# Token-tile projections of the recurrence first, decay sums at other places, forget operations ahead of the taps

## The chip, the core and the metric

The kernel runs on one core of a Trainium2 chip. The core has a matrix engine (TensorE, PE in the profile, with PEld for its weight loads), three engines for elementwise work (VectorE or DVE, ScalarE or ACT, GpSimd or POOL), and a sync engine (SP) that issues most of the transfers. The metric is the device time of one launch in microseconds (us); lower is better.

## The reference

One layer of a decoder for 512 tokens of width 1024, in float32. What matters here is the first block, the mixer: a normalised input is projected once, and three groups of heads use the columns.

```python
y = h @ w_in                       # h: rmsnorm(x), 512 x 1024
fq, fk, fv, ff, hq, hf, hi, hg, cu, cg = split_columns(y, IN_SIZES)
log_f = log_sigmoid(ff + fox_f_bias)          # 8 heads
fo = forgetting_attention(fq, fk, fv, log_f)  # logits + (cumsum(log_f)[t] - cumsum(log_f)[s])
ho = hgrn2_recurrence(hq, hf, hi, lb)         # S_t = diag(f_t) S_{t-1} + (1-f_t) v_t^T, v = hi
ho = rmsnorm(ho) * silu(hg)
a  = causal_depthwise_conv(cu * sigmoid(cg), conv_w, conv_b)   # 31 taps
co = silu(channel_group_norm(a))
x  = x + concat([fo, ho, co]) @ w_out
```

Behind it come cross attention to 256 memory tokens (their keys and values are `mem_n @ w_xkv`) and a mixture of 16 experts, and a last normalisation.

## The kernel before

Each engine has its own program, written out by hand in program order; engines meet through semaphores. Nothing is scheduled by a tool: an instruction that waits holds up all that stands behind it on its engine. There is one order on PE, and the change edits it.

**The start.** SP issues the four token tiles of x (128 tokens x 1024, 512 KB each), then the small parameter rows, then the weights in slots of 512 columns (2 MB each). For each tile ACT squares and sums it, DVE turns the sum into a mean (L982), POOL takes the root (L646), DVE scales the tile into `n_sb` (L993), PE transposes it in two groups of four 128x128 blocks (`turn_group`, L1533), and DVE copies each group times a gain to `hT` (`turn_evac`, L998). Before the change DVE scales tile t and only then empties the turned tile t-1.

**The projections.** `run` counts the groups g: each takes a PSUM bank (`bank_of(g)`, g % 4 for g < 16), raises `proj` when done, and ACT empties it in the order of the list `PROJ` and raises `proj_out`. `across(slot, col)` makes 128 output columns turned, for all 512 tokens (8 matmuls of 128x512, L1722). `input_and_gates(t)` makes hi and ff (264 columns) for one token tile alone (8 matmuls of 128x264, L1754). Since the data are float32, one matmul stands as two in the profile. In the program before, cu, cg, hq and hf (8 groups `across`) come first and the four `input_and_gates` behind them; then `turned_gates` transposes ff (L1761), then the output gates hg, the queries, keys and values of attention, with the work of the recurrence between them.

**DVE behind the projections.** 62 convolution taps (`conv`, L1291 and L1295, two channel groups of 31) in three portions of 26, 14 and 22, with the recurrence's gates (L1311, L1314) and cumulative sums (L1321 to L1327) behind the first portion and the forget gate's work (L1333 to L1339) behind the second; then the attention masks `att_mask` (L1369) and the states of the recurrence, `states_of(p, t)` (L1360, 8 chained steps each). PE makes the products of state step i in `hgrn_u(i)` (L1808); for i >= 2 it waits until DVE has used those of i-2, as the banks alternate.

**The attention loop.** 16 steps u, of 4 query tiles for each of 4 pairs of heads. Step u: `qk(u)` (L1900, and L1902 for the causal mask), `pv(u-3)` (L1924), `pt(u-2)` (L1911, transposes of probabilities), `cum(h)` at the steps of `CUM_AT` (L1889: one matmul spreads head h's cumulative log decay over 128 rows, in bank 7; DVE copies it out in `f_cum`, L1452), `fox_ms` (L1932) after each pair, and at the steps of `KV_AT` one piece of the projection of the memory (L1722 with Dn, 128x256, or L1732, also in bank 7). Bank 7 serves all three, and `bank7_free` waits for the reader of its last content before the next write.

## Time and profile before

| | us |
|---|---|
| median of 3 timed runs (762.08 to 763.15) | 762.64 |
| profiled execution, its own time | 754.83 |
| its span, first to last instruction | 753.1 |
| PE busy | 697.4 (93%) |
| DVE busy | 276.1 (37%) |
| ACT busy | 146.7 (19%) |
| POOL busy | 64.9 (9%) |

Each engine's busy time lies within the span, so the shares don't add up to one. The chain of work that ended last runs over PE for 88% of the span. The profiled execution took 7.8 us less than the median of the timed runs; 1.7 us of its own time lie outside its span.

### The profile page before, as it was taken

The numbers are of one execution on the slowest core, as the hardware profiler recorded it, in microseconds if no ns is written. First come the engines' busy times: TensorE is split into PE (matmuls) and PEld (weight loads), VectorE is DVE, ScalarE is ACT, GpSimd is POOL, SyncE is SP. The second block draws the span as 40 slices with busy tenths as digits, with TensorE's granted clock in tenths as the row PEclk, the third lists the DMA queues.
The fourth block names the chain that finished last, engine by engine and source line by source line (L and its number), as shares of the span: only waits on it lengthen the run. The fifth ranks groups of instructions, "written<-read, shape, count | busy, mean of one in ns | idle before, by whom it ended". The sixth has DMA issues, their size and how long they took to land.

```text
span 753.1 us, 8347 instructions
## 1 busy us (share of the span) xinstructions
PE 697.4 (93%) x3388; PEld 336.5 (45%) x3388; DVE 276.1 (37%) x646; ACT 146.7 (19%) x304; POOL 64.9 (9%) x94
## 2 busy tenths in 40 slices
PE   4999999999989999999999999999955999999992
PEld 3444745454546565454444446544442333333331
DVE  5046996533043544411220005412151732112147
ACT  3100441004262333311100003300010101011112
POOL 2000090420010000000000000000001000000031
PEclk9999999989999999999999999999985999999997
DMA  8730330302221303110009603030089799999562
GB/s 311 251 111 0 113 111 1 112 1 71 98 88 29 112 1 112 52 61 1 0 0 331 215 13 112 2 131 35 29 283 303 237 351 391 376 378 394 194 224 111
DMA packets 65714, 108.21 MB, mean 144 GB/s; under 512 B 5400, under 2 KB 40460, under 8 KB 65676
## 3 DMA queue, kind: packets, MB, share of 16 engines
q1 hardware_dynamic: 62796, 97.19, 37.0%
q0 software_dynamic: 2880, 10.49, 3.8%
q8 instruction: 27, 0.44, 0.2%
q14 instruction: 11, 0.09, 0.0%
HBM read 98.23 MB, written 9.44 MB: 143 GB/s over the span
## 4 chain that ended last, share of the span: by engine, by line
PE 88%; DVE 6%; ACT 2%; DMA 2%; issue 1%; POOL 0%; DVEq 0%; SPq 0%; POOLq 0%
PE bank L1722 27%; PE bank L1980 15%; PE bank L1587 11%; PE bank L1732 8%; PE bank L1615 6%; PE bank L1754 2%; PE bank L2053 2%; PE bank L1768 2%; PE bank L2033 2%; PE bank L1569 2%; PE bank L1924 2%; PE bank L1900 1%; DVE x_sb L1217 1%; PE bank L1533 1%; PE bank L1911 1%
## 5 line engine op out<-in xcount | busy, mean ns | idle before, releaser
L1722 PE MATMUL bank<-hT,W 128*128 128x512 f32 x384 | 168.4, 598 | 1.8 <-DVE hT L998 1.8
L1722 PEld LDWEIGHTS bank<-hT,W 128*128 128x128 f32 x384 | 72.9, 192 | 93.9 <-issue 91.3
L1980 PE MATMUL bank<-W,n_sb 128*128 128x512 f32 x256 | 111.5, 593 | 0.7 <-ACT n_sb L966 0.7
L1980 PEld LDWEIGHTS bank<-W,n_sb 128*128 128x128 f32 x256 | 48.1, 190 | 59.8 <-issue 58.3
L1587 PE MATMUL bank<-W,A 128*32 128x512 f32 x528 | 72.3, 607 | 1.5 <-DVE A L1152 1.5
L1295 DVE SCALAR_TENSOR_TENSOR A<-A,pc 128x511 f32<-128x511 f32 (+29 forms) x60 | 49.4, 824 | 2.1
L1615 PE MATMUL bank<-Dn,A 128*32 128x512 f32 x384 | 43.7, 595 | 0.5 <-ACT A L772 0.5
L1587 PE MATMUL bank<-hT,A 128*32 128x512 f32 x96 | 42.3, 594 | 0.0
L646 POOL TENSOR_TENSOR rstd<-ss,mhalf 128x1 f32<-128x1 f32 x14 | 7.7, 548 | 382.8 <-DVE ss L982 382.8
L1480 DVE TENSOR_TENSOR x_sb<-x_sb,bank 128x512 f32<-128x512 f32 x16 | 11.0, 687 | 79.7 <-PE bank L1980 79.7
L1587 PEld LDWEIGHTS bank<-W,A 128*32 128x32 f32 x528 | 19.2, 112 | 42.6 <-issue 40.4
L1722 PE MATMUL bank<-Dn,W 128*128 128x256 f32 x128 | 33.0, 416 | 4.1 <-DVE A L1452 3.9
L833 ACT ACTIVATE A<-bank 128x512 f32<-128x512 f32 (+1 forms) x22 | 12.2, 556 | 112.0 <-PE bank L1722 91.9
L1161 DVE TENSOR_TENSOR A<-A,bank 128x256 f32<-128x256 f32 x12 | 5.0, 421 | 75.6 <-ACT A L765 75.5
L1722 PEld LDWEIGHTS bank<-Dn,W 128*128 128x128 f32 x128 | 26.0, 208 | 12.4 <-DVE A L1452 8.4
L1420 DVE CUSTOM_DVE_ANT_0 hT<-bank,A 128x128 f32<-128x128 f32 (+3 forms) x32 | 14.4, 487 | 43.2 <-PE bank L1902 43.1
L1732 PE MATMUL bank<-W,hT 128*128 128x512 f32 x64 | 29.9, 623 | 0.0
L1495 DVE TENSOR_REDUCE fmx<-bank 128x1 f32<-128x256 f32 x16 | 6.7, 420 | 62.4 <-PE bank L2033 62.3
L1732 PE MATMUL bank<-W,Dn 128*128 128x512 f32 x64 | 28.2, 594 | 0.0
L743 ACT ACTIVATE A<-x_sb 128x1024 f32<-128x1024 f32 x8 | 8.5, 1057 | 95.8 <-DVE x_sb L1480 95.8
L1360 DVE SCALAR_TENSOR_TENSOR states<-states,Dn,bank 128x64 f32<-128x64 f32 x64 | 18.0, 281 | 19.7 <-PE bank L1808 17.2
L765 ACT ACTIVATE A<-bank 128x256 f32<-128x256 f32 x12 | 4.6, 384 | 100.9 <-PE bank L1587 100.9
(287 smaller groups left out, 796.2 us busy)
## 6 DMA issues: line engine op xcount, KB each, us to landing
Dn<-in_w_down_dram SPq DMA_DIRECT2D x16, 1024.0 KB, 12.3
W<-in_w_gate_dram SPq DMA_DIRECT2D x11, 1024.0 KB, 6.5
W<-in_w_up_dram SPq DMA_DIRECT2D x11, 1024.0 KB, 10.6
W<-in_w_in_dram SPq DMA_DIRECT2D x5, 2048.0 KB, 8.7
W<-in_w_xkv_dram SPq DMA_DIRECT2D x4, 2048.0 KB, 8.1
y_dram<-A SPq DMA_DIRECT2D x10, 512.0 KB, 10.9
W<-in_w_out_dram SPq DMA_DIRECT2D x2, 2048.0 KB, 7.7
W<-in_w_xq_dram SPq DMA_DIRECT2D x2, 2048.0 KB, 8.4
```

Source lines behind the costliest of these rows:

```text
L1295: nc.vector.scalar_tensor_tensor(out=y[:, s:S], in0=a[:, 0:S - s], scalar=pc[:, r:r + 1], in1=y[:, s:S], op0=ALU.mult, op1=ALU.add).then_i ...
L1360: nc.vector.scalar_tensor_tensor(out=states[:, k + 1, :], in0=states[:, k, :], scalar=he4[:, p, k * CHUNK + CHUNK - 1:k * CHUNK + CHUNK], ...
L1569: mm = nc.tensor.transpose(PS[k][:, c * P:(c + 1) * P], src[:, b, (4 * k + c) * P:(4 * k + c + 1) * P], identf[:, :])
L1587: mm = nc.tensor.matmul(PS[2 + b][r, :], xgT[:, b, c, r], gu_at[GU_HOME[e]][:, c, :], start=c == 0, stop=c == DC - 1)
L1615: mm = nc.tensor.matmul(PS[5 + n][r, :], hidT[:, p % 2, k, r], Dn[:, DN_HOME[e], k, 512 * n:512 * n + 512], start=k == 0, stop=k == 1)
L1722: mm = nc.tensor.matmul(bank[0:w, 0:n], lhs, src[:, c, 0:n], start=c == 0, stop=c == DC - 1)
L1732: mm = nc.tensor.matmul(bank[:, 0:w], src[:, c, t * P:(t + 1) * P], W[:, slot, c, col:col + w], start=c == 0, stop=c == DC - 1)
L1754: mm = nc.tensor.matmul(bank[:, 0:IW], hT[:, c, t * P:(t + 1) * P], w_if[:, c, :], start=c == 0, stop=c == DC - 1)
L1768: mm = nc.tensor.matmul(bank[:, :], lhs, hT[:, c, :], start=c == 0, stop=c == DC - 1)
L1924: mm = nc.tensor.matmul(PS[6][64 * a:64 * a + 64, i * P:(i + 1) * P], v[:, j, h * FD:(h + 1) * FD], fpT[a][:, j * P:(j + 1) * P], start=j ...
L1980: mm = nc.tensor.matmul(PS[k % 4][:, :], src[:, c, t * P:(t + 1) * P], W[:, (n_load + n) % SLOTS, c, :], start=first and j == 0, stop=last ...
L2033: mm = nc.tensor.matmul(PS[u % 2][:, 0:M], xqT[:, 2 * h + k, t * P:(t + 1) * P], xkT[:, 2 * h + k, :], start=k == 0, stop=k == 1)
```

## The change

Four edits. (1) SP issues the weights of hi and ff right behind the first tile of x. PE projects hi and ff tile by tile, between the transposes, and only then makes cu, cg, hq and hf. DVE empties each turned tile before it scales the next. `PROJ`, `GROUPS` and the counts that others wait for follow. (2) DVE does the forget gate's operations ahead of the second portion of taps. (3) The first two decay sums go to banks 2 and 3 behind the third group of values, and not to bank 7 in front of the loop; later ones stand right behind `qk`, and their copies on DVE ahead of the copy of `pt`. (4) The pieces of the memory's projection: the first stands ahead of the loop, all after it one place earlier up to step 8, and none at step 9.

```diff
-        KV_AT = [0, 1, 2, 4, 6, 8, 9, 10, 12, 14, 16]
+        KV_AT = [-1, 0, 1, 2, 4, 6, 8, 10, 12, 14, 16]
-        GROUPS = {0: 4, 1: 8, 2: 15, 3: 19, 4: 23, 5: 27, 6: 31, 7: 35, 8: 37, 9: 39, 12: 43, 13: 47}
+        GROUPS = {0: 8, 1: 12, 2: 15, 3: 19, 4: 23, 5: 27, 6: 31, 7: 35, 8: 37, 9: 39, 12: 43, 13: 47}
...
                 if t == 0:
                     sp.dma_start(mixrow[:, :], mix_norm_g[0].rearrange("(c p) -> c p", p=P)).then_inc(mix_in, 16)
+                    sp.dma_start(w_if[:, :, 0:HW], win[:, :, C_HI:C_HI + HW]).then_inc(w_in_slot[2], 16)
+                    sp.dma_start(w_if[:, :, HW:IW], win[:, :, C_FF:C_FF + FH]).then_inc(ff_in, 16)
...
-            for t in range(ST + 1):
-                if t < ST:
-                    normed(dve, 0, t, x_sb, n_sb)
+            for t in range(ST):
+                normed(dve, 0, t, x_sb, n_sb)
...
-                if t >= 1:
-                    turn_tile(dve, 0, t - 1, hT, R_MIX)
+                turn_tile(dve, 0, t, hT, R_MIX)
...
-            conv_some(14)
             dve.wait_ge(proj_out, 13)
...
             nc.vector.tensor_scalar(lfa[:, :], lfa[:, :], 0.0, None, ALU.min).then_inc(lf_dve, 1)
+            conv_some(14)
...
-                nc.vector.tensor_copy(fcum[h % 4], PS[7][:, :]).then_inc(cum_sb, 1)
+                nc.vector.tensor_copy(fcum[h % 4], PS[7 if h > 1 else 2 + h][:, :]).then_inc(cum_sb, 1)
...
+                if u in CUM_AT:
+                    f_cum(CUM_AT[u])
                 if TURN_LAG <= u < UNITS + TURN_LAG:
                     f_pt(u - TURN_LAG)
-                if u in CUM_AT:
-                    f_cum(CUM_AT[u])
...
-            for t in range(ST):
-                turn_tile_pe(0, t, n_sb)
...
-            g = run([across(0, P * c) for c in range(4)], g, 0)
-            g = run([across(1, P * c) for c in range(4)], g, 1)
...
-            pe.wait_ge(hi_in, 4 * 16)
-            g = run([input_and_gates(t) for t in range(ST)], g, 2)
+            turn_tile_pe(0, 0, n_sb)
+            pe.wait_ge(ff_in, 16)
+            for t, ahead in enumerate(([1, 2], [3], [], [])):
+                pe.wait_ge(turn_sb, 2 * t + 2)
+                g = run([input_and_gates(t)], g, 2)
+                for u in ahead:
+                    turn_tile_pe(0, u, n_sb)
+
+            pe.wait_ge(turn_sb, 2 * ST)
+            pe.wait_ge(params_in, 12 * 16)
+            nc.tensor.transpose(PS[4][:, 0:NR], prow[0:NR, :], identf[0:NR, 0:NR]).then_inc(pcol_ps, 1)
+            g = run([across(0, P * c) for c in range(4)], g, 0)
+            pe.wait_ge(pcol, 2)
+            g = run([across(1, P * c) for c in range(4)], g, 1)
+            pe.wait_ge(hi_in, 3 * 16)
...
             g = run([along(1, 2, 0, FW)], g, 5)
+            pe.wait_ge(lf_dve, 5)
+            pe.wait_ge(state_step, 1 + HP * NCH)
+            cum(0)
+            cum(1)
...
-            cum(0)
-            cum(1)
...
+            g = project_memory(0, g)
+            pe.wait_ge(proj_out, XKV0)
             for u in range(UNITS + TURN_LAG):
+                if u == 1:
+                    pe.wait_ge(cum_sb, 2)
                 if u < UNITS:
                     qk(u)
+                if u in CUM_AT:
+                    cum(CUM_AT[u])
```

PE at the start of the program, before. `identf,n_sb` is the turning of the tiles, `W,hT 128x264` is `input_and_gates`, `hT,W` is `across`:

```order
L1707 MATMUL bank<-identf,mixrow 128x8
L1533 MATMUL bank<-identf,n_sb 128x128 x32
L1711 MATMUL bank<-identf,prow 128x108
L1722 MATMUL bank<-hT,W 128x512 x64
L1754 MATMUL bank<-W,hT 128x264 x32
L1761 MATMUL bank<-identf,fft 8x128 x4
```

And in the changed kernel, the same place:

```order
L1707 MATMUL bank<-identf,mixrow 128x8
L1533 MATMUL bank<-identf,n_sb 128x128 x8
L1745 MATMUL bank<-W,hT 128x264 x8
L1533 MATMUL bank<-identf,n_sb 128x128 x16
L1745 MATMUL bank<-W,hT 128x264 x8
L1533 MATMUL bank<-identf,n_sb 128x128 x8
L1745 MATMUL bank<-W,hT 128x264 x16
L1773 MATMUL bank<-identf,prow 128x108
L1715 MATMUL bank<-hT,W 128x512 x64
L1752 MATMUL bank<-identf,fft 8x128 x4
```

The 32 matmuls of 128x264 now stand in three pieces between the turnings and ahead of the 64 of `across`; the second piece stands behind the turnings of two tiles.

PE from the third group of values up to the second attention step, before. `n_sb,identf` is a decay sum, `Dn,W` a piece of the memory's projection, `A 128x128` the scores of step 0:

```order
L1732 MATMUL bank<-W,hT 128x512 x8
L1533 MATMUL bank<-identf,Dn 128x128 x8
L1732 MATMUL bank<-W,hT 128x512 x8
L1533 MATMUL bank<-identf,Dn 128x128 x8
L1889 MATMUL bank<-n_sb,identf 128x512 x2
L1900 MATMUL bank<-A 128x128 x2
L1902 MATMUL bank<-causal,identb 128x128 x2
L1722 MATMUL bank<-Dn,W 128x256 x8
L1900 MATMUL bank<-A 128x256 x2
L1902 MATMUL bank<-causal,identb 128x128 x2
L1889 MATMUL bank<-n_sb,identf 128x512
```

And in the changed kernel:

```order
L1725 MATMUL bank<-W,hT 128x512 x8
L1881 MATMUL bank<-n_sb,identf 128x512 x2
L1533 MATMUL bank<-identf,Dn 128x128 x8
L1725 MATMUL bank<-W,hT 128x512 x8
L1533 MATMUL bank<-identf,Dn 128x128 x8
L1715 MATMUL bank<-Dn,W 128x256 x8
L1908 MATMUL bank<-A 128x128 x2
L1910 MATMUL bank<-causal,identb 128x128 x2
L1715 MATMUL bank<-Dn,W 128x256 x8
L1908 MATMUL bank<-A 128x256 x2
L1910 MATMUL bank<-causal,identb 128x128 x2
L1881 MATMUL bank<-n_sb,identf 128x512
```

The two decay sums moved ahead of the memory's turnings, and a piece of the memory's projection took their place in front of the scores.

DVE from the second cumulative sum of the recurrence's gates on, before, in two pieces (12 more of the 14 taps stand between them in the program):

```order
L1321 SCALAR_TENSOR_TENSOR Dn<-scanmask,Dn 128x512
L1324 TENSOR_TENSOR Dn<-Dn 128x512
L1327 TENSOR_TENSOR Dn<-Dn 128x512
L1295 SCALAR_TENSOR_TENSOR A<-A,pc 128x486
```

```order
L1295 SCALAR_TENSOR_TENSOR A<-A,pc 128x504
L1333 MEMSET n_sb 8x512
L1334 TENSOR_SCALAR n_sb<-n_sb,fbias 8x512
L1336 SCALAR_TENSOR_TENSOR n_sb<-n_sb 8x512
L1339 TENSOR_SCALAR n_sb<-n_sb 8x512
L1342 MEMSET Dn 128x2048
```

And in the changed kernel:

```order
L1321 SCALAR_TENSOR_TENSOR Dn<-scanmask,Dn 128x512
L1324 TENSOR_TENSOR Dn<-Dn 128x512
L1327 TENSOR_TENSOR Dn<-Dn 128x512
L1332 MEMSET n_sb 8x512
L1333 TENSOR_SCALAR n_sb<-n_sb,fbias 8x512
L1335 SCALAR_TENSOR_TENSOR n_sb<-n_sb 8x512
L1338 TENSOR_SCALAR n_sb<-n_sb 8x512
L1295 SCALAR_TENSOR_TENSOR A<-A,pc 128x486
```

The four operations on 8x512 moved from behind 14 taps to in front of them.

## Rows read from the trace of the kernel before

**Rows 1.** Waits of PE, whole kernel; us in total, times, longest.
```profile
PE bank L1533 <- DVE n_sb L993: 4.9, 4, 2.6
...
PE bank L1722 <- DVE A L1452: 3.9, 5, 0.8
```

**Rows 2.** Timeline of PE: start, length, engine, line, work, idle before.
```profile
7.03 1.97 PE L1533 MATMUL bank<-identf,n_sb 128*128 128x128 f32 x8 [2.58 <-DVE n_sb L993]
...
18.21 56.61 PE L1722 MATMUL bank<-hT,W 128*128 128x512 f32 x128 [0.82 <-DVE hT L998]
74.66 14.40 PE L1754 MATMUL bank<-W,hT 128*128 128x264 f32 x64
89.42 0.60 PE L1761 MATMUL bank<-identf,fft 128*8 128x128 f32 x4 [0.36 <-ACT fft L825]
...
219.70 1.04 PE L1533 MATMUL bank<-identf,Dn 128*128 128x128 f32 x8
```

**Rows 3.** Timeline of PE's weight loads, as the first projection starts.
```profile
20.05 0.34 PEld L1722 LDWEIGHTS bank<-hT,W 128*128 128x128 f32 x1 [0.52 <-issue]
20.91 0.29 PEld L1722 LDWEIGHTS bank<-hT,W 128*128 128x128 f32 x1 [0.52 <-issue]
21.44 0.19 PEld L1722 LDWEIGHTS bank<-hT,W 128*128 128x128 f32 x1 [0.24 <-issue]
```

**Rows 4.** Timeline of all engines, the second token tile.
```profile
6.95 1.06 ACT L743 ACTIVATE n_sb<-x_sb 128x1024 f32<-128x1024 f32 x1 [1.58 <-DMA x_sb<-in_x_dram]
...
8.21 0.15 DVE L982 TENSOR_SCALAR ss<-ss 128x1 f32<-128x1 f32 x1 [1.16 <-ACT n_sb L743]
...
9.03 0.75 DVE L993 TENSOR_SCALAR n_sb<-x_sb,rstd 128x1024 f32<-128x1024 f32 x1 [0.67 <-POOL rstd L646]
...
9.70 1.28 DVE L998 TENSOR_TENSOR hT<-bank,pc 128x512 f32<-128x512 f32 x2
```

**Rows 5.** Timeline of SP's DMA issues.
```profile
6.90 1.68 SPq L586 DMA_DIRECT2D W<-in_w_in_dram  x2
...
13.09 5.28 SPq L581 DMA_DIRECT2D W<-in_w_in_dram  x1
...
22.14 2.74 SPq L584 DMA_DIRECT2D W<-in_w_in_dram  x1
```

**Rows 6.** Windows: stretch, us, busy by engine, clock, DMA share, GB/s.
```profile
23.00:24.00 1.00, 1.00 (x3) 0.38 (x2) 0.00 (x0) 0.00 (x0) 0.00 (x0) 1.00 1.08 207
```

**Rows 7.** Timeline of DVE: decay gates, taps, masks and states.
```profile
75.49 0.55 DVE L1311 TENSOR_SCALAR A<-A,lbv 128x512 f32<-128x512 f32 x1 [5.79 <-ACT A L833]
...
96.71 1.76 DVE L1342 MEMSET Dn<- 128x2048 f32 x1 [0.94 <-ACT Dn L847]
...
102.15 22.12 DVE L1295 SCALAR_TENSOR_TENSOR A<-A,pc 128x503 f32<-128x503 f32 x22
126.42 1.34 DVE L1369 COPY_PREDICATED Dn<-chunkmask,bank 128x512 f32<-128x512 int32 x2 [2.15 <-PE bank L1794]
134.99 5.09 DVE L1360 SCALAR_TENSOR_TENSOR states<-states,Dn,bank 128x64 f32<-128x64 f32 x16 [7.23 <-PE bank L1808]
```

**Rows 8.** Timeline of PE: state products, and attention's start and tenth step.
```profile
143.70 1.03 PE L1808 MATMUL bank<-A,Dn 128*64 128x512 f32 x4
...
221.87 1.09 PE L1889 MATMUL bank<-n_sb,identf 8*128 8x512 f32 x2 [1.14 <-DVE Dn L998]
223.75 1.12 PE L1889 MATMUL bank<-n_sb,identf 8*128 8x512 f32 x2 [0.78 <-DVE A L1452]
...
225.65 5.41 PE L1722 MATMUL bank<-Dn,W 128*128 128x256 f32 x16
...
233.74 3.72 PE L1722 MATMUL bank<-Dn,W 128*128 128x256 f32 x16 [0.78 <-DVE A L1452]
...
286.23 5.41 PE L1722 MATMUL bank<-Dn,W 128*128 128x256 f32 x16 [0.78 <-DVE A L1452]
```

**Rows 9.** Windows (columns as in rows 6), in the tenth attention step.
```profile
288.00:290.00 2.00, 2.00 (x6) 1.55 (x5) 0.00 (x0) 0.00 (x0) 0.00 (x0) 0.50 0.00 0
```

More of the change, by code:

```diff
@@ L292, in build @@
         hi_in = sem("hi_in")
+        ff_in = sem("ff_in")
         ff_sb = sem("ff_sb")
@@ L805, in experts_act @@
                                      accum_out=ss[:, NORM0[3] + ST + t:NORM0[3] + ST + t + 1]).then_inc(fin_sq, 1)
-        PROJ = ([("t", cuT[:, c], ACT.Copy) for c in range(2)] + [("t", cgT[:, c], ACT.Sigmoid) for c in range(2)]
+        PROJ = ([("hv", hv[:, t], ACT.Copy) for t in range(ST)] + [("t", cuT[:, c], ACT.Copy) for c in range(2)] + [("t", cgT[:, c], ACT.Sigmoid) for c in range(2)]
                 + [("t", hqT[:, c], ACT.Copy) for c in range(2)] + [("t", hfT[:, c], ACT.Sigmoid) for c in range(2)]
-                + [("hv", hv[:, t], ACT.Copy) for t in range(ST)] + [("ff", lfa[:, :], ACT.Copy)] + [("t", hgT[:, c], ACT.Silu) for c in range(2)]
+                + [("ff", lfa[:, :], ACT.Copy)] + [("t", hgT[:, c], ACT.Silu) for c in range(2)]
                 + [("q", qT[:, c], ACT.Copy) for c in range(4)] + [("t", kT[:, c], ACT.Copy) for c in range(4)]
@@ L824, in proj_evac @@
                     if kind == "hv":
-                        nc.scalar.activation(fft[:, g - 8, :], PS[bank_of(g)][:, HW:IW], ACT.Copy).then_inc(ff_sb, 1)
+                        nc.scalar.activation(fft[:, g, :], PS[bank_of(g)][:, HW:IW], ACT.Copy).then_inc(ff_sb, 1)
                     if kind == "ff":
@@ L833, in proj_evac @@
                         nc.scalar.activation(dst, PS[bank_of(g)][:, 0:w], fn).then_inc(proj_out, 1)
-            proj_evac(0, 8)
+            proj_evac(0, 12)
             for p in range(HP):
@@ L839, in _ @@
                 nc.scalar.activation(hgl[:, p], hfT[:, p], ACT.Ln).then_inc(hg_log, 1)
-            proj_evac(8, 13)
+            proj_evac(12, 13)
             for p in range(HP):
@@ L923, in kv_evac @@
                     act.wait_ge(ho_step, 2 * HP)
+                    act.wait_ge(co_done, 2)
                 k = g - XKV0
@@ L1707, in _ @@
             nc.tensor.transpose(PS[0][:, 0:DC], mixrow[:, :], identf[0:DC, 0:DC]).then_inc(pcol_ps, 1)
-            for t in range(ST):
-                turn_tile_pe(0, t, n_sb)
-            pe.wait_ge(params_in, 12 * 16)
-            nc.tensor.transpose(PS[1][:, 0:NR], prow[0:NR, :], identf[0:NR, 0:NR]).then_inc(pcol_ps, 1)
-            pe.wait_ge(turn_sb, 2 * ST)
-            pe.wait_ge(pcol, 2)
             def across(slot, col, w=P, src=None, n=S):
@@ L1866, in _, with bank7_free, cum @@
                 nc.tensor.matmul(PS[4 + p][:, :], half64[:, :], he3[:, p], start=True, stop=True).then_inc(ho_ms, 1)
+            bank7 = []
+            def bank7_free():
+                if bank7:
+                    pe.wait_ge(*bank7.pop())
+            def cum(h):
+                if h > 1:
+                    bank7_free()
+                nc.tensor.matmul(PS[7 if h > 1 else 2 + h][:, :], identf[0:FH, h:h + 1].to_broadcast([FH, P]), lfa[:, :],
+                                 start=True, stop=True).then_inc(cum_ps, 1)
+                if h > 1:
+                    bank7.append((cum_sb, h + 1))
             g = run([along(1, 2, 0, FW)], g, 5)
+            pe.wait_ge(lf_dve, 5)
+            pe.wait_ge(state_step, 1 + HP * NCH)
+            cum(0)
+            cum(1)
             pe.wait_ge(ho_sb, HP)
@@ L1875, in _ @@
                 turn_group(pe, 1, 1, k, PS[6 + k], mem_sb)
-            bank7 = []
-            def bank7_free():
-                if bank7:
-                    pe.wait_ge(*bank7.pop())
-            def cum(h):
-                if h == 0:
-                    pe.wait_ge(lf_dve, 5)
-                bank7_free()
-                nc.tensor.matmul(PS[7][:, :], identf[0:FH, h:h + 1].to_broadcast([FH, P]), lfa[:, :],
-                                 start=True, stop=True).then_inc(cum_ps, 1)
-                bank7.append((cum_sb, h + 1))
             def qk(u):
@@ L1941, in _, with project_memory @@
             pe.wait_ge(turn_sb, TURN0[2])
-            cum(0)
-            cum(1)
+            def project_memory(k, g):
+                bank7_free()
+                if k < DC:
+                    g = run([across(2 + k // 4, P * (k % 4), src=memT, n=M)], g, 6 + k // 4)
+                else:
+                    q = (k - DC) // MT
+                    g = run([along(q, (k - DC) % MT, 0, 512, src=memT)], g, 8 + q)
+                bank7.append((proj_out, g))
+                return g
+            g = project_memory(0, g)
+            pe.wait_ge(proj_out, XKV0)
             for u in range(UNITS + TURN_LAG):
+                if u == 1:
+                    pe.wait_ge(cum_sb, 2)
                 if u < UNITS:
                     qk(u)
+                if u in CUM_AT:
+                    cum(CUM_AT[u])
                 if u >= PV_LAG:
@@ L1956, in _ @@
                 if u in KV_AT:
-                    k = KV_AT.index(u)
-                    bank7_free()
-                    if k < DC:
-                        g = run([across(2 + k // 4, P * (k % 4), src=memT, n=M)], g, 6 + k // 4)
-                    else:
-                        q = (k - DC) // MT
-                        g = run([along(q, (k - DC) % MT, 0, 512, src=memT)], g, 8 + q)
-                    bank7.append((proj_out, g))
+                    g = project_memory(KV_AT.index(u), g)
             def logits_of(t):
```

14 lines of the change are left out of this document (4 added, 10 removed).

## The prediction

> **What bounds the kernel now.** From the page I take that PE is busy for 93% of the span and that 88% of the chain that ended last is its work, so I read the waits of PE first, over the whole kernel. Where the change edits, two stand out: 4.9 us in 4 times for scaled tiles at the start, and 3.9 us in 5 times for DVE's copies of decay sums [rows 1]. Then the timelines of the places the change touches: the start [rows 2], where PE works from 7.03 but makes its first projection only from 18.21; the middle up to 220, where PE has next to no wait; and the attention loop. A second loss is TensorE's clock. Weight loads of one shape follow each other by 0.86 us at 20.05 and 20.91, and from 21.44 by 0.19 + 0.24 = 0.43 [rows 3]. The first 3.1 us of the projection thus ran at half pace, at 1.2 and not 2.4 GHz, and lost 1.55 us. (The windows print a granted clock of 1.00 for this first stretch; I go by the pace.) The turning of a tile shows the same: 8 transposes take 1.97 us at 7.03 and 1.04 at 219.70 [rows 2].
>
> **Part 1, the start.** PE's work up to the turned gates at 89.42 is the same before and after; only waits and half pace count. I follow the new order. Tile 0 is turned from 7.03 to 9.00. DVE empties its two groups right behind (1.28 for both [rows 4]), done by 9.8; before, tile 1's scaling stood in between. `input_and_gates(0)` starts at 9.9. One tile is 14.40 / 4 = 3.6 us at full pace [rows 2]; with the same 3.1 us at half pace as at 18.21 it takes 5.1 and ends at 15.0. Tile 1, long scaled, is turned by 16.0. Now the price of DVE's new order: the second group is emptied by 16.7, then mean, root and scaling, 8.21 to 9.78 before or 1.6 us [rows 4], so tile 2 is ready at 18.3. PE idles 2.3 us, since `input_and_gates(1)` stands behind this turning in the program. I take it that the clock falls there, because gaps of 1.14 and 0.78 at 222 were enough to bring a piece at half pace behind them [rows 8]. Then tile 2's turning takes 2.0 (to 20.4) and `input_and_gates(1)` 5.1 (to 25.5). Tile 3, ready at 20.4 + 0.7 + 1.6 = 22.7, is turned by 26.5 without a wait. The last two tiles take 7.1, to 33.6; the parameters' transpose (108 columns and its start) I put at 0.5. `across` starts at 34.1. Its 64 matmuls took 56.61 [rows 2], 1.55 of it half pace; at full pace the turned gates stand at 34.1 + 54.9 = 89.0 against 89.42, of which 0.36 was a wait for ff that is now long out. **Gain 0.4.** Bounds: if the clock holds over the gap, 1.0 and 1.5 less, gain 3.0; if all of `input_and_gates(0)` runs at half pace, 7.2 instead of 5.1, loss 1.7.
>
> The Trainium skill says that the halved clock is the default and that activity releases it, and that the point of release varies from run to run (TensorE: Matmul & The Clock Gate, What's actually happening, and What you observe). The rows agree with the first. By the second the 3.1 us are one draw of several, which is why both bounds stay open here.
>
> The transfers could spoil this. SP now issues hi (1 MB) and ff (1024 rows of 32 bytes) ahead of tiles 1 to 3. ff's issue took 5.28 us before, but SP was then held by a full queue: two whole slots of as many rows each took 1.68 together, and 64 KB in 128 rows took 2.74 in the same jam [rows 5]. So I take 0.8 for each. While ff was under way the rate fell to 207 GB/s for a microsecond [rows 6], near 350 beside it, so ff costs at most 1 us. Tile 0, hi and ff are in by about 8; tile 1 by about 9.4 instead of 6.95 [rows 4]. hi and ff are wanted at 9.9; tile 1 at 15.0 less 1.6 less 1.3 for its square, 12.1. **Cost 0**, hidden by tile 0's projection; beyond 1.9 and 2.7 us of cover, each microsecond late is one of PE's.
>
> Rows below 512 bytes miss the engines' line rate, says the Trainium skill (DMA: Bandwidth & Descriptors, Specifications), which speaks against putting ff ahead of x; the slice at 207 GB/s agrees, and gives the price.
>
> **Part 2, DVE late in the middle.** The last gate hf is now ready for DVE at 34.1 + 54.9 + 0.7 = 89.7, not at 75.49. DVE's chain from there is the same work in another order (cumulative sums, forget operations, 36 taps): 75.49 to 102.15 + 22.12 = 124.27, 48.8 us, less the 0.94 of idle that the taps now fill [rows 7]. It ends at 137.6, 13 us later, while PE is not later at all. The masks of pair 0 (1.34) and two state steps (5.09) follow, so the banks come free at 137.6 + 6.5 = 144.1. DVE had 2.15 and 7.23 us of idle around these [rows 7], which swallow most. PE wants the second bank for `hgrn_u(3)` at 143.70 [rows 8] less 0.4 from part 1: **a wait of 0.8**, and queued behind it are a projection and the products and states of pair 1; they have slack again, so it is paid once. Bounds: 0, and 2.8 if POOL's products beside other taps cost DVE 2 us more. The forget operations ahead of the taps cost 0; behind 14 taps (up to 14 us by [rows 7]) they would have held ACT's exponential and the hg gates queued behind it.
>
> **Part 3, the entry of attention.** From 221.87 to 230.99 PE did two decay sums, waited 0.78, made the scores of step 0 and the memory's first piece in 5.41, where a piece at full clock takes 3.72 [rows 8]. The two sums now stand ahead of the memory's turnings, cost there what they cost here, and their copies are hidden by the first piece. The wait of 1.14 for the turned memory stays. Without the second gap I expect the clock to hold: **gain 0.8 + 1.7 = 2.5**; 0.8 if it falls all the same.
>
> **Part 4, the loop.** Five times PE waited 0.78 between a decay sum and the memory's piece behind it [rows 1, 8]. At step 1 nothing stands between them now either: that wait stays. At step 2 a small `pt` covers 0.3 to 0.4. At steps 5 and 9 no piece follows, and at 6 and 10 `pv` and `pt` (over 0.8 together) cover it: 3 x 0.78. **Gain 2.7**, bounds 1.9 and 3.1. `f_cum` ahead of `f_pt` makes one copy 0.7 later, which the next step's `qk` and sum (1.1 alone) hide. The piece at 286.23 took 5.41, at clock 0.50 [rows 8, 9], behind such a wait; whether this half pace goes with the wait I leave at half: **gain 0.8**, between 0 and 1.7.
>
> **Sum.** -0.4 + 0.8 - 2.5 - 2.7 - 0.8 = -5.6. The profiled execution goes from 754.83 to 749.2. The median of the runs lies 7.8 above that execution; I let it move by as much: 762.64 - 5.6 = 757.0. What stands behind the loop only shifts; no wait for weights stands there that an earlier start could uncover.
>
> **The rivals.**
> (a) The clock is kind: it holds over the gap at the start and in step 10, and all bounds fall well: -3.0 + 0 - 2.5 - 3.1 - 1.7 = -10.3, so 752.3. Against it: at 222 smaller gaps were enough. Chance 0.15.
> (b) The clock gives nothing back in attention; half pace moves to another place: -0.4 + 0.8 - 0.8 - 2.7 = -3.1, so 759.5. For it: what is left around the sums are still thin matmuls and a gap of 1.14. Chance 0.2.
> (c) Slower: the interleaving keeps the clock down through all four tiles. They cost 14.4 more than at full pace, and three turnings 3.0; 4.0 of this is in the sum. 757.0 + 13.4 = 770.4. It decides from 12 us of added half pace on (a loss of 5.6 is half of that). Against it: tiles 2 and 3 are 7 us of unbroken matmuls, and 3.1 us were enough at 18.21. Chance 0.04.
> (d) The new order of transfers is late: each of the two issues takes some 5 us, tile 1 is issued at 12 and lands at 15, its turning comes 2.7 us late, and a further spell at half pace costs 2: 757.0 + 4.7 = 761.7. Against it: the 2.74 us row. Chance 0.08.
> (e) DVE's lateness costs 2.8 and the start loses 1.7: 757.0 + 2.0 + 2.1 = 761.1. Chance 0.08.
>
> **How the numbers follow.** The remaining 0.45 is my forecast's, with 755 to 758.8 for its own range. The range from 752.3 to 760.6 leaves out (c), half of (a), and most of (d) and (e), under 0.2. A measurement of this kernel can tell 0.2%, 1.5 us, from no change, so faster means below 761.1. Above it or at it lie (c) and parts of (d) and (e): faster 0.87, same 0.07, slower 0.06.
>
> **What would show it.** In the changed profile `across` starts near 34 (31.5 or 36 by the clock); the pieces of 264 columns take 5.1, 5.1 and 7.1 us, with 2.3 us of idle ahead of tile 2's turning; PE waits under 1 us for DVE's states near 143; the memory's first piece takes 3.7 and not 5.4; and PE waits 1.2 and not 3.9 us for L1452. I am wrong if PE waits for weights or for x at the start, if the states hold PE for several microseconds, or if new stretches at clock 0.50 stand in the loop.

## The result, and the profile after

The changed kernel took 765.12 us (median of 12 runs, 764.07 to 766.13), and the kernel before, run beside it, 761.99: a ratio of 1.0048, with a 95% interval of 1.0031 to 1.0064. It is slower by half a per cent, where 757.0 was forecast. The profiled execution took 765.17 us (span 763.4, mean clock 0.959).

The waits of PE in the changed kernel (us in total, times, longest), against [rows 1]:

```profile
PE bank L1615 <- ACT A L773: 5.1, 1, 5.1
...
PE bank L1533 <- DVE n_sb L995: 5.0, 2, 2.5
PE bank L1812 <- DVE states L1360: 4.6, 2, 3.5
...
PE bank L1715 <- DVE A L1452: 3.2, 4, 1.0
```

Two rows are new. The third, for DVE's states, is the loss. The first, for ACT in the last expert pass, is not the change's: the kernel before shows it too when it is run and profiled again on one chip (5.1), and no kernel shows more than 0.5 on the two others. The profile from which the prediction was made had 0.5 there; on which chip it was taken is not known.

To see where the time went, I compare the timeline of PE with that of the kernel before, profiled again, at four places that both have: the turned gates, the first half-weighted sum of the convolution's variance, the start of the product with `w_out`, and the end. The first row is the profile from which the prediction was made. The other three are from one chip, and the last of them is an experiment that is told below.

| us from the span's start | gates | variance | `w_out` | span |
|---|---|---|---|---|
| before, first profile | 89.42 | 172.23 | 329.82 | 753.1 |
| before, again | 89.31 | 170.52 | 330.73 | 760.8 |
| after | 87.00 | 177.40 | 331.57 | 763.4 |
| last taps split | 86.85 | 169.62 | 323.87 | 753.7 |

Against the second row the start gained 2.3, the middle lost 9.2 (90.40 for 81.21), attention and what lies around it gained 6.0 (154.17 for 160.21), and 1.8 was lost behind it. The sum is +2.6, as the spans say.

A stage of one and the same kernel is not that constant. In the first profile of the kernel before, the middle took 82.81 and attention 157.59, since the stretches at half pace lay elsewhere; against it the middle lost 7.6 and attention gained 3.4. So both sizes have a spread: 7.6 to 9.2 for the loss, 3.4 to 6.0 for the gain.

**The start**, PE's timeline (start, length, engine, line, work, idle before), against [rows 2]:

```profile
7.11 1.97 PE L1533 MATMUL bank<-identf,n_sb 128*128 128x128 f32 x8 [2.49 <-DVE n_sb L995]
9.90 6.20 PE L1745 MATMUL bank<-W,hT 128*128 128x264 f32 x16 [0.83 <-DVE hT L1000]
15.94 1.04 PE L1533 MATMUL bank<-identf,n_sb 128*128 128x128 f32 x8
19.49 1.06 PE L1533 MATMUL bank<-identf,n_sb 128*128 128x128 f32 x8 [2.51 <-DVE n_sb L995]
20.39 3.73 PE L1745 MATMUL bank<-W,hT 128*128 128x264 f32 x16
...
24.83 7.29 PE L1745 MATMUL bank<-W,hT 128*128 128x264 f32 x32
...
32.05 8.33 PE L1715 MATMUL bank<-hT,W 128*128 128x512 f32 x19
```

The first piece ran longer at half pace than forecast (6.20 for 5.1), but the clock stayed up over 2.51 us of idle: the turning behind it took 1.06, not 2.0, and the next piece 3.73. This is so in 9 of the 11 profiles with the new start. In the two others, of experiments told below, the piece behind the same wait ran at half pace for a while, much as forecast; here with POOL's products held:

```profile
18.68 1.06 PE L1534 MATMUL bank<-identf,n_sb 128*128 128x128 f32 x8 [2.51 <-DVE n_sb L996]
19.58 5.41 PE L1746 MATMUL bank<-W,hT 128*128 128x264 f32 x16
```

**The middle**, DVE's timeline, against [rows 7]:

```profile
87.83 0.55 DVE L1311 TENSOR_SCALAR A<-A,lbv 128x512 f32<-128x512 f32 x1 [5.79 <-ACT A L834]
...
99.21 7.28 DVE L1295 SCALAR_TENSOR_TENSOR A<-A,pc 128x486 f32<-128x486 f32 x5
106.42 1.49 DVE L1291 TENSOR_SCALAR A<-A,pc 128x512 f32<-128x512 f32 x1
107.94 8.87 DVE L1295 SCALAR_TENSOR_TENSOR A<-A,pc 128x511 f32<-128x511 f32 x8
...
120.73 19.44 DVE L1295 SCALAR_TENSOR_TENSOR A<-A,pc 128x503 f32<-128x503 f32 x22
140.09 1.32 DVE L1369 COPY_PREDICATED Dn<-chunkmask,bank 128x512 f32<-128x512 int32 x2
141.31 10.28 DVE L1360 SCALAR_TENSOR_TENSOR states<-states,Dn,bank 128x64 f32<-128x64 f32 x32
```

and what PE does there:

```profile
133.31 7.13 PE L1715 MATMUL bank<-hT,W 128*128 128x512 f32 x16
143.93 1.49 PE L1812 MATMUL bank<-Dn 128*64 128x512 f32 x4 [3.49 <-DVE states L1360]
146.53 1.97 PE L1812 MATMUL bank<-A,Dn 128*64 128x512 f32 x4 [1.11 <-DVE states L1360]
148.44 3.09 PE L1798 MATMUL bank<-Dn 64*128 64x128 f32 x16
151.46 8.73 PE L1715 MATMUL bank<-hT,W 128*128 128x512 f32 x16
```

The taps end at 140.17, so no bank is free before the states. PE waits 3.49 + 1.11 = 4.60, and then runs slowly. The same rows at full pace, in the kernel before, take 1.08, 1.03, 1.71 and 7.13: behind the waits 0.41 + 0.94 + 1.38 + 1.60 = 4.33 more. Together that is 8.9 of the 9.2. (The first profile of the kernel before also has these rows at full pace. Its middle is 1.6 longer because more of the work behind them ran at half pace.)

Why DVE's chain is longer than the 47.9 of the prediction shows beside POOL. Its timeline in the changed kernel:

```profile
94.31 1.61 POOL L689 TENSOR_TENSOR Dn<-Dn 128x512 f32<-128x512 f32 x1 [72.18 <-ACT Dn L848]
...
110.21 2.93 POOL L707 TENSOR_TENSOR A<-A,chunkcol 128x512 f32<-128x512 f32 x2
132.61 2.69 POOL L707 TENSOR_TENSOR Dn<-A,chunkcol 128x512 f32<-128x512 f32 x2 [19.47 <-PE bank L1812]
```

and, of the kernel before profiled again, POOL and DVE:

```profile
94.11 1.28 POOL L688 TENSOR_TENSOR Dn<-Dn 128x512 f32<-128x512 f32 x1 [80.66 <-ACT Dn L847]
...
134.93 2.04 POOL L706 TENSOR_TENSOR Dn<-A,chunkcol 128x512 f32<-128x512 f32 x2 [21.98 <-PE bank L1808]
```

```profile
82.25 3.75 DVE L1295 SCALAR_TENSOR_TENSOR A<-A,pc 128x486 f32<-128x486 f32 x5
...
86.50 6.23 DVE L1295 SCALAR_TENSOR_TENSOR A<-A,pc 128x511 f32<-128x511 f32 x8
...
134.88 5.10 DVE L1360 SCALAR_TENSOR_TENSOR states<-states,Dn,bank 128x64 f32<-128x64 f32 x16 [7.23 <-PE bank L1808]
```

POOL's first products start at 94 in both kernels, since they hang on ACT. Only DVE moved. Before, its 14 taps were done at 92.7 and took about 0.75 each; now they run from 99.2 to 116.8, mostly beside POOL (94.3 to 113.1), and take 1.1 to 1.5. Before, POOL's second piece met the state steps, which it does not slow; now it meets the last taps. By the rows, the 14 taps cost 7.1 more (17.6 for 10.5) and the forget operations 1.5 more (4.4 for 2.9), while the last 22 taps took 2.7 less and the two operations ahead of them 1.6 less. With 0.2 more of idle this makes 4.5.

**Attention**, PE and then DVE, against [rows 8]:

```profile
230.69 3.69 PE L1715 MATMUL bank<-Dn,W 128*128 128x256 f32 x16 [1.15 <-DVE Dn L1000]
...
268.82 3.72 PE L1715 MATMUL bank<-Dn,W 128*128 128x256 f32 x16 [1.02 <-DVE A L1452]
...
289.65 3.72 PE L1715 MATMUL bank<-Dn,W 128*128 128x256 f32 x16 [1.02 <-DVE A L1452]
```

```profile
267.47 0.69 DVE L1441 COPY n_sb<-bank 128x512 f32<-128x512 f32 x1 [0.59 <-PE bank L1932]
268.08 0.68 DVE L1452 COPY A<-bank 128x512 f32<-128x512 f32 x1
```

The pieces that took 5.4, the first and the one of step 10, take 3.7, here and in every profile with the new order. In 4 of the 11 another piece is at half pace in its place, for instance the third with the attention edits alone:

```profile
235.24 5.41 PE L1723 MATMUL bank<-Dn,W 128*128 128x256 f32 x16 [0.79 <-DVE A L1453]
```

At steps 6 and 10, where I had counted the copy as hidden, DVE makes the copy of the pair's output first; that one waits for `pv`, and the copy of the sums is queued behind it. Windows of 20 us (busy PE, PEld, DVE, ACT, POOL; clock; DMA share; GB/s) give the clock, of the changed kernel and then of the kernel before, profiled again:

```profile
220.00:240.00 20.00, 18.85 (x79) 11.76 (x78) 6.84 (x19) 7.70 (x14) 0.00 (x0) 1.00 0.39 110
...
280.00:300.00 20.00, 18.82 (x117) 11.35 (x116) 10.91 (x37) 8.02 (x23) 0.00 (x0) 1.00 0.27 97
```

```profile
220.00:240.00 20.00, 17.26 (x65) 10.55 (x64) 6.84 (x24) 4.42 (x12) 0.00 (x0) 0.83 0.36 110
...
280.00:300.00 20.00, 19.06 (x98) 11.97 (x97) 8.69 (x30) 7.00 (x20) 0.00 (x0) 0.91 0.30 106
```

### The profile page after: what moved, and what is told of

It is laid out like the page before. It is cut to its first block, busy times and chain, and to the rows that moved or that the text cites. A ratio compares the mean times of both kernels' runs of the same rounds, so it can differ in the third digit from the quotient of the medians.

```text
span 763.4 us, 8351 instructions
## 1 busy us (share of the span) xinstructions
PE 700.2 (92%) x3388; PEld 335.8 (44%) x3388; DVE 280.2 (37%) x646; ACT 147.3 (19%) x304; POOL 66.8 (9%) x94
## 4 chain that ended last, share of the span: by engine, by line
PE 80%; DVE 13%; ACT 2%; issue 2%; DMA 1%; another core or an unknown queue 1%; POOL 0%; DVEq 0%; POOLq 0%
PE bank L1715 21%; PE bank L1992 14%; PE bank L1587 11%; PE bank L1725 8%; PE bank L1615 6%; DVE A L1295 4%; PE bank L1745 2%; PE bank L2065 2%; PE bank L2045 2%; PE bank L1569 2%; PE bank L1533 2%; PE bank L1932 2%; PE bank L1908 1%; DVE x_sb L1219 1%; PE bank L1831 1%
## 5 line engine op out<-in xcount | busy, mean ns | idle before, releaser
L1715 PEld LDWEIGHTS bank<-hT,W 128*128 128x128 f32 x384 | 73.0, 192 | 93.0 <-issue 91.6
L1295 DVE SCALAR_TENSOR_TENSOR A<-A,pc 128x511 f32<-128x511 f32 (+29 forms) x60 | 52.9, 882 | 2.1
L1615 PE MATMUL bank<-Dn,A 128*32 128x512 f32 x384 | 46.6, 628 | 5.1 <-ACT A L773 5.1
L1587 PEld LDWEIGHTS bank<-W,A 128*32 128x32 f32 x528 | 19.5, 113 | 43.4 <-issue 41.2
L1715 PE MATMUL bank<-Dn,W 128*128 128x256 f32 x128 | 29.5, 384 | 4.4 <-DVE A L1452 3.2
L834 ACT ACTIVATE A<-bank 128x512 f32<-128x512 f32 (+1 forms) x22 | 12.1, 557 | 110.3 <-PE bank L1715 90.4
L1715 PEld LDWEIGHTS bank<-Dn,W 128*128 128x128 f32 x128 | 23.7, 190 | 9.2 <-DVE A L1452 4.8
L1615 PEld LDWEIGHTS bank<-Dn,A 128*32 128x32 f32 x384 | 11.8, 114 | 31.3 <-issue 26.0
## 6 DMA issues: line engine op xcount, KB each, us to landing
W<-in_w_up_dram SPq DMA_DIRECT2D x11, 1024.0 KB, 10.7
```

The lines of the kernel that those rows point to most:

```text
L1295: nc.vector.scalar_tensor_tensor(out=y[:, s:S], in0=a[:, 0:S - s], scalar=pc[:, r:r + 1], in1=y[:, s:S], op0=ALU.mult, op1=ALU.add).then_i ...
L1587: mm = nc.tensor.matmul(PS[2 + b][r, :], xgT[:, b, c, r], gu_at[GU_HOME[e]][:, c, :], start=c == 0, stop=c == DC - 1)
L1615: mm = nc.tensor.matmul(PS[5 + n][r, :], hidT[:, p % 2, k, r], Dn[:, DN_HOME[e], k, 512 * n:512 * n + 512], start=k == 0, stop=k == 1)
L1715: mm = nc.tensor.matmul(bank[0:w, 0:n], lhs, src[:, c, 0:n], start=c == 0, stop=c == DC - 1)
```

## The experiments

Line numbers of the kernels differ by one here and there. They ran on three chips, four to a chip, each against runs of the kernel before on the same chip: it takes 762.0 us on the first, 754.5 on the second and 754.9 on the third. Across chips I therefore compare ratios: the kernel's median over that of the kernel before on the same chip, with the 95% interval in brackets.

### First chip: which half of the change costs

**The kernel before, again.**

> The kernel before, unchanged, to get a second profile of it. The profiled execution of the kernel before was 7.2 us below its median of 761.99, and its last passes over the experts hold no wait of PE for ACT, where the changed kernel waits 5.1 us (and then runs 2.9 us longer at half pace). Theory A (that wait belongs to both kernels, the first profile happened to miss it): the profile lies near 762 and holds the 5 us wait in the last pass. Theory B (the change brings that wait): the profile shows no such wait, and lies near 755 or loses the time elsewhere.

Measured: 762.78, ratio 0.9998 (0.997 to 1.0025). Its profile is the "before, again" above.

**The attention edits alone** (the sums at their new places, `f_cum` ahead of `f_pt`; start, transfers and forget operations as before).

> Only the edits of attention (decay sums early and in banks 2 and 3, memory pieces one place earlier), the start and the forget operations as before. Theory A (the attention edits gain, the middle loses): 4.5 us faster than before, 757.5. Rival C (the gain in attention is given back behind it, by the clock or by the waits in the last pass): within 1.5 us of before. Rival D (the attention edits themselves lose): slower.

Measured: 758.67, ratio 0.9959 (0.9942 to 0.9975), or 3.3 us less than before (1.9 to 4.4), where 4.5 was expected. From the variance to `w_out` it takes 154.27, within 0.1 of the changed kernel. Its start was 2.3 us later than that of the kernel before in the profiled execution, with the old order of both, so 2.3 is what a start can vary by. The eleven profiles with the new start have the turned gates at 86.3 to 87.9, the three with the old one at 89.3, 89.4 and 91.6: the start did gain, and at least 1.4.

**The start and the forget operations alone** (attention as before).

> Only the edits of the start and of the forget operations, attention as before. Theory A: start gains 2.4, then PE waits 4.6 us for the states and works some 4 us longer at half pace behind that: 6 to 8 us slower than before, 769. Rival C: 3 us slower, as the whole change, 765, with attention worth nothing.

Measured: 769.77, ratio 1.0101 (1.0071 to 1.0131), 7.8 us more than before, with 4.8 us of waits for the states. The two halves multiply to 1.006, near the 1.0048 of the whole, so nothing shows that they work on each other, and the loss is in this half. Beside it the whole change, with attention's edits added, is 4.7 us faster.

**The last taps split.** The changed kernel, in which DVE makes 13 of its last 22 taps ahead of the masks and states of pair 0 and of pair 1's mask, and 9 behind them:

```diff
-            conv_some(len(taps))
+            conv_some(13)
...
             att_mask(1)
+            conv_some(len(taps))
```

> The changed kernel, but the last 22 taps of DVE split: 13 ahead of the masks and states, 9 behind the masks of pair 1. The first state steps then come about 6.7 us earlier. Theory A (DVE's lateness is the loss): the waits of 3.5 and 1.1 us for states go, the half pace behind them too, and the kernel runs 7 to 9 us faster than the change, about 757, and faster than before by 4 to 5. Rival C (the half pace and the tail decide, not the wait): 4.6 us faster than the change at most, about 761. Rival E (the 9 late taps hold up the convolution's means): a new wait of PE for DVE near 158 takes back more than 2 us.

Measured: 754.79, ratio 0.9899 (0.9873 to 0.9926). DVE's timeline:

```profile
120.59 9.96 DVE L1295 SCALAR_TENSOR_TENSOR A<-A,pc 128x503 f32<-128x503 f32 x13
130.47 1.33 DVE L1369 COPY_PREDICATED Dn<-chunkmask,bank 128x512 f32<-128x512 int32 x2
132.42 5.10 DVE L1360 SCALAR_TENSOR_TENSOR states<-states,Dn,bank 128x64 f32<-128x64 f32 x16 [0.63 <-PE bank L1813]
141.35 5.10 DVE L1360 SCALAR_TENSOR_TENSOR states<-states,Dn,bank 128x64 f32<-128x64 f32 x16 [3.83 <-PE bank L1813]
```

PE has no wait for the states any more, no new one near 158, and the middle takes 82.77 where the changed kernel takes 90.40. The 14 taps are as slow beside POOL as ever. The masks start 9.6 us earlier (130.47 for 140.09): 6.8 are the nine taps now behind them, and 2.7 come because POOL's second piece meets the state steps again and not taps (13 and 9 take 9.96 + 6.80, the 22 took 19.44). This is the test of the cause: DVE does the same operations, only in another order, and the kernel is 10.3 us faster, more than the 7 to 9 expected. The middle has 7.6 of them; behind `w_out` another 2.0 went (429.83 for 431.83), where two pieces behind waits that both kernels have lost less at half pace (8.40 for 9.77, and 5.84 for 6.56). That part is not shown to be the edit's doing.

### Second chip: POOL, the forget operations, and two repairs

**POOL's products held.** The changed kernel, in which POOL waits for DVE's first 14 taps:

```diff
+            pool.wait_ge(conv_y, 40)
             for p in range(HP):
```

> This is the changed kernel (765.12) with POOL's products held until DVE's first 14 taps (about 40 counted) are done; they then run beside the last 22 taps. In the changed kernel the taps beside POOL's products took 7.28 for 5 and 8.87 for 8, or 1.1 to 1.46 each, against some 0.75 to 0.77 each for those alone. Theory (DVE and POOL slow each other where both read SBUF): the 14 taps now take 0.77 each, some 10.7 us and not 17.6, and the taps behind them are slowed by about as much instead: DVE's chain ends as late as before, within 2 us, so the wait for the states stays near 4.6 and the time at 763 to 767; if POOL's products themselves are now late for PE, more. Rival (the slow taps are slow for their own shape or for what they wait on, not for POOL): the 14 taps still take 17 us with POOL idle, and the chain ends where it did.

Measured: 757.37, ratio 1.0046 (1.0026 to 1.0066). DVE:

```profile
97.55 3.74 DVE L1296 SCALAR_TENSOR_TENSOR A<-A,pc 128x486 f32<-128x486 f32 x5
...
101.78 6.23 DVE L1296 SCALAR_TENSOR_TENSOR A<-A,pc 128x511 f32<-128x511 f32 x8
...
113.26 26.70 DVE L1296 SCALAR_TENSOR_TENSOR A<-A,pc 128x503 f32<-128x503 f32 x22
139.88 1.32 DVE L1370 COPY_PREDICATED Dn<-chunkmask,bank 128x512 f32<-128x512 int32 x2
```

With POOL idle the same 14 taps take 3.74 + 0.54 + 6.23 = 10.5 and not 17.6, and the 22 behind them, now beside POOL, 26.7 and not 19.4. The slowness goes with POOL, so the rival falls. The chain ends where it did (139.88 against 140.09), PE waits 3.3 for the states, and the time is that of the changed kernel. Holding POOL only moves its cost along DVE's chain.

**The forget operations back behind the 14 taps.**

```diff
+            conv_some(14)
             dve.wait_ge(proj_out, 13)
...
-            conv_some(14)
```

> This is the changed kernel (765.12) with the forget operations put back behind the 14 taps. Theory of the prediction: the forget operations feed ACT's exponential and the gates queued behind it on ACT; 14 taps, some 18 us beside POOL's products, put these that much later, ACT empties the banks of the next projections late, and PE waits several microseconds near 115: 770 or more, with a new wait for ACT in PE's list. Rival: ACT and PE have slack there, and DVE's sum of work is the same, so the wait for the states near 143 stays at 4.6 and the time stays: 764 to 766. Second rival: the forget operations, no longer beside POOL's first products, run faster and the chain on DVE ends earlier: below 764.

Measured: 756.97, ratio 1.0044 (1.0026 to 1.0062). DVE, and then PE:

```profile
93.97 8.31 DVE L1295 SCALAR_TENSOR_TENSOR A<-A,pc 128x486 f32<-128x486 f32 x5
102.20 1.49 DVE L1291 TENSOR_SCALAR A<-A,pc 128x512 f32<-128x512 f32 x1
103.72 10.64 DVE L1295 SCALAR_TENSOR_TENSOR A<-A,pc 128x511 f32<-128x511 f32 x8
...
120.82 16.79 DVE L1295 SCALAR_TENSOR_TENSOR A<-A,pc 128x503 f32<-128x503 f32 x22
```

```profile
120.98 9.60 PE L1716 MATMUL bank<-hT,W 128*128 128x512 f32 x16 [5.78 <-ACT A L834]
```

The mechanism that the prediction named is there: ACT is held, and PE waits 5.78 for it and loses 9.60 - 7.03 = 2.57 at half pace behind it. But PE, 8.4 us late, then finds the states done, and the other wait is gone. The time comes out as with the changed kernel, for another reason: this wait or that one, not both. None of my three theories had this trade.

**The sums' copy first.** The kernel with the split taps, and in DVE's order of the loop `f_cum` ahead of `f_out`:

```diff
-                if pair_end(u) is not None:
-                    f_out(pair_end(u))
                 if u in CUM_AT:
                     f_cum(CUM_AT[u])
+                if pair_end(u) is not None:
+                    f_out(pair_end(u))
```

> This is the kernel with the split taps (754.79, no wait for the states) with one more edit: in DVE's order of the loop the copy of the decay sums stands ahead of the copy of the pair's output. In the changed kernel PE waits 3.2 us in 4 times for the copies of decay sums, 1.02 us of it at each of the two steps at which the output's copy stands ahead of the sums' on DVE and itself waits 0.59 for the product of the value tiles. Theory: these two waits are the order's, so both go and PE waits about 1.2 us in 2 times there: about 752.8, 2.0 below the split taps. Rival: something else of the step (the scores' product, or a half pace that moves) takes the place: the two waits go or shrink, but the time stays at 754 to 755.5. Second rival: the output's copy, now later, holds the banks of the next pair and PE waits for the copy instead: 755 or more.

Measured: 744.86, ratio 0.9887 (0.9844 to 0.9931). PE's list of waits now has

```profile
PE bank L1716 <- DVE A L1453: 1.2, 2, 0.8
```

So the two waits of 1.02 were the order's. Whether they show in the time, this run can't tell from the 0.9899 of the split taps on the first chip; the last experiment is the test of it.

**Stores first.** The kernel with the split taps, and SP issues the store of an expert pass's rows ahead of the loads of down weights:

```diff
-                    if DN_REFILL[p - 1]:
...
                     if p <= NP - LATE:
...
                         sp.dma_start(y_rows[p - 1], ysb[:, (p - 1) % 2]).then_inc(y_stored[(p - 1) % 2], 16)
+                    if DN_REFILL[p - 1]:
```

> This is the kernel with the split taps (754.79) with one more edit: SP issues the store of an expert pass's rows ahead of the loads of down weights that stand behind the same pass, where before it issued the loads first. In the last pass PE waits 5.1 us for ACT, which waits for its half of the output buffer, whose earlier store is late; behind the wait a piece takes 6.56 and not 3.64. Theory: the store is late because the weight loads stand ahead of it in SP's queue; issued first it is out in time, the wait of 5.1 and the 2.9 of half pace behind it go: 754.8 - 8.0 = 746.8. Rival: the store waits for ACT and DVE before it can be issued, so now the loads are held behind it, and PE waits for down weights by about as much: 753 to 757, or slower. Second rival: the wait is not the store's; then nothing changes, 754.8 and the same 5.1 in the profile.

Measured: 747.54, ratio 0.9935 (0.9907 to 0.9963). The experiment could not decide: on this chip the wait it was to remove is 0.5 us in every kernel, with the edit or without.

### Third chip: again, side by side

**The changed kernel, again.**

> The changed kernel once more, beside the three below on the same chip. On the first chip it took 1.0048 of the time of before. Kernels with one edit undone came out at 1.0044 and 1.0046 on a chip on which the kernel before takes 754.5 and not 762, so that they can only be compared with it over the ratio. Theory: the ratio is the program's, and it comes out at 1.003 to 1.007 here too. Rival: the ratio hangs on the chip, because the wait of 5.1 us in the last expert pass is there on one and not on the other: below 1.003.

Measured: 757.53, ratio 1.0046 (1.003 to 1.0063), on a chip without the late wait. The rival falls, and the two ratios of 1.0044 and 1.0046 of the second chip are indeed those of the changed kernel. Its waits for the states are 4.4.

**The split taps, again.**

> The changed kernel with its last 22 taps split around the masks and states, once more, on the chip of the three others. Theory: 0.988 to 0.992 of before, as on the first chip (0.9899), and 1.4% under the changed kernel. Rival: part of it was the chip's, 0.993 or more.

Measured: 748.62, ratio 0.9918 (0.9895 to 0.9942): 8.9 below the changed kernel. That equals the 8.9 of waits and half pace found in the middle, but in part by chance: by these two profiles the middle took 79.56 for 90.27, 10.7 less. The same kernel's middle took 82.77 on the first chip, with more of it at half pace.

**Stores first, again.**

> Split taps, and the store of an expert pass ahead of the loads of down weights. On the second chip it gave 0.9935 of before, and the wait of 5.1 us that it was to remove was in no profile there. Theory: where the chip shows the wait without the edit, the edit removes it and the kernel comes out 5 to 8 us below the split taps alone; where it does not, the two are the same within 1.5 us. Rival: the stores ahead of the loads cost something of their own, 2 to 3 us (0.9935 against 0.9899), and it is slower than the split taps on either chip.

Measured: 748.45, ratio 0.9921 (0.9896 to 0.9946). The medians with and without the edit are 0.2 us apart, so the edit costs nothing that these runs can show. What it would do on the first chip stays open.

**All three repairs.**

> Split taps, stores first, and in the loop the copy of the decay sums ahead of that of the pair's output. In the profile with that last edit PE waits 1.2 us in 2 times for the copies and not 3.2 in 4. Theory: 2 us below the kernel with split taps and stores first. Rival: the removed waits do not show in the time, within 1 us of it, because half pace or another wait of the loop takes their place.

Measured: 745.80, ratio 0.9879 (0.985 to 0.9908), 2.65 below the kernel with stores first and split taps alone; 2.0 was expected. The runs scatter by as much (745.06 to 747.08 against 747.01 to 750.06) but hardly overlap, and in the profiles attention takes 151.61 for 154.17. This kernel is 1.2% faster than the one before and by the medians 1.5% faster than the changed one.

## Why the prediction was wrong

**What failed is part 2**, "a wait of 0.8" for the states, with 2.8 as the worst. It was 4.6, and two things in its working were off.

- The chain of DVE was moved as a block of 47.9 us. It took 140.17 - 87.83 = 52.3. [rows 7] held the hint: 22 taps in 22.12 are 1.0 each, where the taps ahead of them took 0.75, and I did not read POOL's timeline beside them. Had I, it would have shown POOL's products at 94 to 113 and again from 135, fixed by ACT and PE, and DVE's free taps sliding under them. The bound "if POOL's products beside other taps cost DVE 2 us more" had the right mechanism at half its size: 4.4. The forget operations, put at a cost of 0, are in this with 1.5. That DVE began 1.9 us earlier than forecast (87.83 for 89.7) did not help, because PE came earlier by as much: it could have made the products of `hgrn_u(3)` at 141.3 and not 143.3. So the delay was 0.8 + 4.4, and PE made the product at 146.53, 5.2 late, of which 4.6 were idle and the rest half pace.
- The wait was priced alone. Behind 4.6 us of waits PE ran at half pace, which cost 4.3 more. The prediction charged just this at the start and in attention and forgot it here. With it, the unfavourable bound would have been near 5 (an estimate: 2.8 at the same rate).

The held products, the split taps and the forget operations show the chain link by link: POOL slows the taps, the late taps hold the states, the states hold PE, and with another order of the same taps the loss is gone.

**Part 1** was right in its order and wrong in size, the safe way: 2.3 gained for 0.4 forecast. "I take it that the clock falls there" was the step that failed here: it held over 2.51 us, as in 9 of 11 profiles, and fell behind the same wait in 2. The transfers were hidden, as said, though later than said: SP's two issues took 0.40 and 0.58, and tile 1 was squared from 10.88, not 9.4, but before the 12.1 at which it was wanted. That the forget operations behind the taps would hold ACT was right by mechanism, yet worth nothing in this kernel.

**Part 3** came as forecast: the first piece of the memory took 3.69, and the wait of 1.14 stayed.

**Part 4** was wrong on its waits: 3.2 us in 4, not 1.2. The step was "at 6 and 10 `pv` and `pt` (over 0.8 together) cover it". I looked at what PE does between the sum and the piece, and not at what DVE has queued ahead of the copy; with that order turned the waits were the 1.2 that I had given. The clock made up for it. In waits for copies the changed kernel saves 4.7 - 3.2 = 1.5; by the windows it saves 0.17 x 20 = 3.4 and 0.09 x 20 = 1.8 of lost pace. That is 6.7, against 6.0 by the timeline, and parts 3 and 4 had forecast 2.5 + 2.7 + 0.8 = 6.0. In this pair of profiles the sum was right because two errors cancelled, and even that is luck. Against the profile from which the forecast was made the stage gained 3.4: there 1.6 less was lost at half pace ahead of 203 us, where the change edits nothing, and 1.0 less behind it. In the timed runs attention's edits are worth 3.3 alone and 4.7 on top of the other half. So 6.0 was too much rather than right, and the half pace that moved to another piece in 4 of 11 profiles is what rival (b) named.

**The base.** The forecast was made against one execution of 754.83 and shifted by 7.8 to the median. That gap is mostly the late wait: 5.12 for 0.5, and 5.92 for 3.64 in the piece behind it, 6.9 together. It shifts both kernels, as assumed. Of the 1.8 lost behind `w_out` in the comparison above, 0.6 is that piece's (6.56 against 5.92), and 1.2 is that of the first product behind PE's wait of 8.5 us near 570 (9.77 against 8.57). Both kernels have both waits; only the length at half pace behind them differs.

So: +9.2 where +0.8 was forecast (+7.6 against the other profile), -2.3 where -0.4 was, and -3.3 to -6.0 where -6.0 was. None of the rivals was it. Rival (e) named the right place at about a third of its price, and no case carried DVE's lateness beyond 2.8.

## What to carry to other kernels

When a block of one engine's work is moved in time, lay every other engine's timeline beside its new place: what it will run beside is as much a part of its price as its own length. Price a wait of PE together with the half pace that may follow it: each microsecond waited cost nearly two at the states, 1.4 with the forget operations late (5.78 + 2.57), and mostly just one at the start. Take the spread of a stage from two profiles of the same kernel before a gain of a few microseconds is read from it. And in a chain that feeds a waiting engine, put the work that nobody waits for behind the work that somebody does: nine taps moved behind the states were worth more than all the rest of the change.

## What the hardware did that I had not expected

**VectorE and GpSimd slow each other, by the kind of operand.** A tap (two tensors from SBUF, 128 x 503) takes 0.76 alone (22 in 16.79) and 1.4 to 1.7 beside POOL's products (5 in 8.31; of the 8 in 10.64 the last two ran mostly alone). The first tap of a channel group (L1291), with one tensor from SBUF, takes 0.54 alone and 1.49 beside them. POOL's product of 128 x 512 takes 1.27 beside no taps and about 1.7 beside them. The state steps, which read one operand from a bank, are not slowed: 16 take 5.10 beside POOL (from 134.88) and without it (from 173.46, both in the kernel before, profiled again), and POOL's own pair takes 2.04 there and 2.7 to 2.9 beside taps. The Trainium skill (SBUF — State Buffer, SBUF: two separate sides) says that the two engines share one pair of SBUF ports, wanted by a VectorE operation with two SBUF inputs, against a GpSimd operation that reads SBUF, or by one in a two-port mode, and that whoever starts first holds it for the whole instruction while the other fully blocks. The rows agree on which operations with two SBUF inputs collide, and the two engines do take turns: with the forget operations late, POOL's 12 products ran from 93.58 to 112.25, 18.7 us, and DVE started 12 operations in them and finished some 11.6. But one after the other, at 8 x 1.27 + 4 x 1.02 and 10.6 x 0.75 + 0.54, these would take 22.7 (an estimate from the rows alone). Some 4 us, or 0.3 per turn, do overlap; whether the block is shorter than an instruction's row or the rows hold more than the block, the runs do not settle.

**The clock does not fall by the length of a gap alone.** Over 2.51 us of idle at 17 to 19.5 it stayed up in 9 of 11 profiles and fell in 2. It stayed up behind the waits of 1.02 in the changed loop, and was down behind waits of 1.14 and 0.78 in the attention of the kernel before and behind 3.49 and 1.11 in the middle of the changed one. What tells these apart the runs do not settle.

**The same program has a wait on one chip and not on another.** PE's wait of 5.1 to 5.4 us in the last expert pass stands in the five profiles of the first chip that are told here (the changed kernel's among them, whose timed runs of the kernel before agree with that chip) and in none of the eight of the other two, where the kernel before is 1% faster. The first profile of the kernel before lacks it too; its 754.83 is the time of the other two chips, but its chip is not known, so it may also be that the wait comes and goes on one chip.
